# Eight bursts of small products in a gated recurrence gathered into two

## The chip, the cores and the metric

The kernel runs on one core of one Trainium2 chip. The metric is the time of one execution on the device in microseconds (us); less is better. Runs of this kernel lie within some 0.06% of each other, so a difference of about 0.2% (1.9 us) is what a measurement can tell from none.

## The reference, cut to what matters

Two transformer blocks with 256 tokens and a width of 1024, in float32. The change touches one mixer of the first block, a gated linear recurrence with 4 heads of 128 channels, worked in chunks of 64 tokens:

```python
f = lb + (1.0 - lb) * jax.nn.sigmoid(f_logit)
qh, kh, ih = heads(silu(q)), heads(1.0 - f), heads(i)
G = jnp.cumsum(heads(jnp.log(f)), axis=3)
def step(S, inp):
    qc, kc, ic, Gc = inp
    diff = Gc[:, :, :, None, :] - Gc[:, :, None, :, :]
    decay = jnp.exp(jnp.where(causal, diff, -jnp.inf))
    A = jnp.einsum('bhtc,bhsc,bhtsc->bhts', qc, kc, decay)
    o = einsum('bhts,bhsv->bhtv', A, ic) + einsum('bhtc,bhcv->bhtv', qc * jnp.exp(Gc), S)
    S_new = S * jnp.exp(G_last)[..., None] + einsum('bhsc,bhsv->bhcv', kc * jnp.exp(G_last - Gc), ic)
```

## The kernel before

Nearly all the work is projections of 256 tokens by streamed weights. A weight unit (1 MB) is loaded by SyncE's queue into one of three `raw` buffers, ScalarE rounds it to float32r (`Wh`, in `hi_to`, L1104), VectorE makes the rest (`Wl`, in `lo_to`, L1620), and TensorE sums three wide products for each (`three`, L418). Each engine's program is written out by hand in one order; semaphores join them. The two rings `Wh` and `Wl` hold three units, so ScalarE may start on unit u+2 of this stage when TensorE has ended unit u-1.

The attention matrix `A` of the recurrence is made without a chunk loop. For a block of 128 tokens it is split by halves of 1, 2, 4, ... 64 tokens: seven levels. In level n the later half of each pair of halves looks at the earlier half. `level_sub(n)` on VectorE writes differences of `G` into a buffer `E`, `level(n)` on ScalarE takes their exponential in place, `level_mul(n)` on VectorE multiplies them by keys and queries, `level_products(n)` on TensorE multiplies the halves (L698), and `level_out(n)` on VectorE copies what belongs to `A` out of the PSUM bank, for levels 0 to 4 into `Near`, for 5 and 6 into `Am`. The diagonal comes from `own_products` (L688) and `near_out`. ScalarE later copies `Near` into `Am` (L1264, four instructions). Then `cross_products` (L707) needs the chunk-to-chunk factors that `chunk_sub`, an exponential (L1271) and `chunk_mul` (L1866, L1867) make in `E1`, and `hgrn_out` (L724, L725) multiplies by the values.

None of this fills TensorE, so it is woven into the six gate projections: twelve weight units, u = 0 to 11, of 24 wide products each. After unit u TensorE calls `levels_after(u)`. At u = 0 that is the diagonal, at u = 1 to 7 level u-1. The loops `for u in range(12)` of ScalarE and VectorE have the steps that go with it in the same count. `gate_out(j)` on ScalarE reads a finished half of a gate out of PSUM, which frees its bank for a later unit. The levels take turns in two buffers `E`, and their products in the four PSUM banks of `T`. Products of the levels use 32 columns of the array at a time (64 in level 6), the projections 128. Each call on float32 data stands twice in the trace, with two loads of weights.

Of the kernel before, what the change touches and what calls it, by code (L numbers as in the profile page):

```python
# [9 lines left out]
ACT = mybir.ActivationFunctionType  # L10
# [5 lines left out]
HALVES = (1, 2, 4, 8, 16, 32, 64)  # L16
# [124 lines left out]
def heads(x, n):  # L141
    return x.rearrange("p (h d) -> p h d", h=n)


def build(nc, plan, I, out):
    ctx = ExitStack()
    with ctx:
        def sb(name, n, dt=F32, parts=128):
            return ctx.enter_context(nc.sbuf_tensor(name, [parts, n], dt))
# [19 lines left out]
        HG = sb("HG", 5 * 1024)  # L169
        Am, Ax = sb("Am", 1024), sb("Ax", 512)  # L170
        Iv, Sg, Vt, Vm = sb("Iv", 1024), sb("Sg", 1024), sb("Vt", 1024), sb("Vm", 1024)
        P = [sb(f"P{i}", 512) for i in range(2)]
        PT = [sb(f"PT{i}", 512) for i in range(2)]
        Near = PT[0][:, 0:256]
        onesr, DH, DL = sb("onesr", 128, F32R), sb("DH", 256, F32R), sb("DL", 256, F32R)
# [68 lines left out]
            return VT[:, ROWS[name] + i:ROWS[name] + i + 1]  # L244

        Q, K, G, E0, E1 = (HG[:, 1024 * j:1024 * j + 1024] for j in range(5))
        E = (E0, E1)

        forget_own, forget_keys = Iv, (Vm[:, :], G)
        forget_sums = nc.dram_tensor("forget_sums", [8, 256], F32).ap()  # L250
# [45 lines left out]
        def full(key):  # L296
            return ps_full[at[key][0]], at[key][1]

        def free(key):
            return ps_free[at[key][0]], at[key][2]  # L300
# [98 lines left out]
        def pe_program(pe):  # L399
# [280 lines left out]
            def own_products():  # L680
                b = T.take()
                pe.wait_ge(k_made, 1)
                pe.wait_ge(q_made, 2)
                t = take("kq", b)
                for q in range(8):
                    for x in range(0, 128, 32):
                        c = slice(q * 128 + x, q * 128 + x + 32)
                        ins = pe.matmul(t[x:x + 32, q * 32:q * 32 + 32], K[:, c], Q[:, c], start=True, stop=True)  # L688
                ins.then_inc(ps_full[b], 1)

            def level_products(n):
                pe.wait_ge(dec_mul, 2 * n + 2)
                b = T.take()
                t = take(("lv", n), b)
                for q in range(8):
                    s = E[n % 2][:, q * 128:q * 128 + 128]
                    for x, w, a, z in LEVELS[n]:
                        ins = pe.matmul(t[x:x + w, q * w + w - z:q * w + w], s[:, x:x + w], s[:, x + a:x + a + z],  # L698
                                        start=True, stop=True)
                ins.then_inc(ps_full[b], 1)  # L700
# [25 lines left out]
                    ins.then_inc(ps_full[6 + m], 1)  # L726

            def levels_after(u):
                if u == 0:
                    own_products()  # L730
                elif u < 8:
                    level_products(u - 1)
                elif u == 10:
                    hgrn_out()

# [356 lines left out]
        def act_program(act):  # L1092
# [134 lines left out]

            def level(n):
                act.wait_ge(dec_sub, 2 * n + 2)
                act.activation(E[n % 2], E[n % 2], ACT.Exp).then_inc(dec_exp, 1)  # L1230

            def gate_sigmoid(j):
                g = BIGT[:, j * 1024:j * 1024 + 1024]
# [12 lines left out]
            def gate_out(u):  # L1246
                c, m = u // 2, u % 2
                half_scaled(BIGT[:, c * 1024:c * 1024 + 1024], ("gate", c), m, rs0)

            level(0)  # L1250
            for u in range(12):
                hi_to(gate_unit(u) + 2)
                if u >= 2 and u % 2 == 0 and u < 8:
                    gate_out(u - 1)
                if u in (5, 6):
                    mem_squares(u - 5)
                if 1 <= u <= 6:
                    level(u)
                elif u == 7:
                    gate_out(6)  # L1260
                    gate_out(7)
                    act.wait_ge(*free(("lv", 4)))
                    for x in range(0, 128, 32):
                        act.activation(heads(Am[x:x + 32, :], 8)[:, :, x:x + 32], heads(Near[x:x + 32, :], 8),  # L1264
                                       ACT.Copy).then_inc(near_placed, 1)
                    for j in range(4):
                        gate_sigmoid(j)
                elif u == 8:
                    gate_out(8)
                    act.wait_ge(ch_sub, 4)  # L1270
                    act.activation(E1, E1, ACT.Exp).then_inc(ch_exp, 1)  # L1271
                    gate_out(9)
                elif u == 9:
                    act.wait_ge(*full("ax"))
                    act.wait_ge(lam_made, 1)
                    act.activation(Ax[:, :], bank[at["ax"][0]][:, :], ACT.Copy).then_inc(*emptied("ax"))
                elif u == 10:
                    for m in range(2):
                        act.wait_ge(*full(("ho", m)))
                        act.activation(P[m][:, :], bank[6 + m][:, :], ACT.Square).then_inc(ho_sq, 1)  # L1280
                if u in (1, 3, 5, 11):
                    gate_out(u - 1)
# [327 lines left out]
        def dve_program(dve):  # L1610
# [188 lines left out]

            def level_sub(n):  # L1800
                half = HALVES[n]
                v, g = (x.rearrange("p (a c b) -> p a c b", c=2, b=half) for x in (E[n % 2], G))
                end = g[:, :, 0, half - 1:half].to_broadcast([128, 512 // half, half])
                if n >= 2:
                    dve.wait_ge(*full(("lv", n - 2)))
                dve.tensor_tensor(v[:, :, 0, :], end, g[:, :, 0, :], ALU.subtract).then_inc(dec_sub, 1)
                if half < 64:
                    dve.tensor_tensor(v[:, :, 1, :], g[:, :, 1, :], end, ALU.subtract).then_inc(dec_sub, 1)
                else:
                    dve.tensor_copy(v[:, :, 1, :], g[:, :, 1, :]).then_inc(dec_sub, 1)  # L1810

            def level_mul(n):
                v, kv, qv = (x.rearrange("p (a c b) -> p a c b", c=2, b=HALVES[n]) for x in (E[n % 2], K, Q))
                dve.wait_ge(dec_exp, n + 1)
                dve.tensor_tensor(v[:, :, 0, :], v[:, :, 0, :], kv[:, :, 0, :], ALU.mult).then_inc(dec_mul, 1)
                dve.tensor_tensor(v[:, :, 1, :], v[:, :, 1, :], qv[:, :, 1, :], ALU.mult).then_inc(dec_mul, 1)
# [68 lines left out]
            for u in range(12):  # L1885
                lo_to(gate_unit(u) + (1 if u else 2))
                if 1 <= u < 7:
                    level_sub(u)
                if u == 0:
                    near_out("kq", 0, 0)  # L1890
                elif u < 7:
                    level_out(u - 1)
                    level_mul(u)
                elif u == 7:
                    level_out(6)
                elif u == 8:
                    chunk_sub()
                    lo_to(gate_unit(u) + 2)
                    chunk_mul()
                elif u == 10:  # L1900
                    hgrn_sums()
                if u:
                    lo_to(gate_unit(u) + 2)
# [660 lines left out]
```

## Time and profile before

| | us |
|---|---|
| median of three runs | 944.49 |
| lowest, highest | 944.22, 944.8 |
| profiled execution, whole | 944.71 |
| its span, first to last instruction | 942.8 |
| TensorE busy in the span | 935.6 |
| VectorE, ScalarE busy | 695.3, 526.8 |

The whole time of the profiled execution is 1.9 us more than its span. Busy shares count overlapping instructions once; the end of a matmul is modelled, so what a product costs is read from the distance of starts, not from its own duration.

### The profile page before, as it was taken

Reading aid. Unit: us, or ns where it says so; the run is one execution under the profiler, and the core shown is the slowest. Engines: PE = TensorE matmul, PEld = TensorE weight load, DVE = VectorE, ACT = ScalarE, POOL = GpSimd, SP = SyncE. Lnnn points to the kernel's source line nnn. Section 1 sums busy time; section 2 is a strip of 40 time slices with the busy share of each in tenths; the row PEclk is TensorE's granted clock in tenths of the full one; section 3 lists DMA queues with packets and bytes.
Section 4 is the critical chain, followed back from the end, with each engine's and each line's share of the span. In section 5 each row is a group of like instructions: output and inputs, shape, how many; then the busy total and the mean of one; then the engine's idle time right before and its main releaser. Section 6 shows DMA issues by size and latency. Waiting matters only on the chain.

```text
span 942.8 us, 13704 instructions
## 1 busy us (share of the span) xinstructions
PE 935.6 (99%) x5478; PEld 802.8 (85%) x5478; DVE 695.3 (74%) x1001; ACT 526.8 (56%) x673; POOL 80.9 (9%) x150
## 2 busy tenths in 40 slices
PE   9999999999999999999999999999999999999997
PEld 9988888888888888888888888888887888888886
DVE  6788668778768777788886757578878677576675
ACT  6676766654446556555655445356655465354544
POOL 1010228182100000000000000000003000000000
PEclk9999999999999999999999999999999999999999
DMA  9844555334564554556364554653534445646441
GB/s 360 332 157 161 176 182 221 135 135 161 186 239 179 184 193 166 217 179 223 135 230 172 197 205 178 223 179 135 182 134 171 164 144 213 222 155 221 160 179 45
DMA packets 26111, 175.10 MB, mean 186 GB/s; under 512 B 3256, under 2 KB 3520, under 8 KB 6080
## 3 DMA queue, kind: packets, MB, share of 16 engines
q1 hardware_dynamic: 25168, 170.15, 49.6%
q10 hardware_dynamic: 880, 4.07, 1.2%
q8 instruction: 44, 0.72, 0.3%
q14 instruction: 19, 0.16, 0.0%
HBM read 173.15 MB, written 1.06 MB: 185 GB/s over the span
## 4 chain that ended last, share of the span: by engine, by line
PE 99%; DVE 0%; ACT 0%; issue 0%; POOL 0%; ACTq 0%; POOLq 0%
PE ps L418 47%; PE ps L425 29%; PE ps L429 15%; PE ps L548 1%; PE ps L646 1%; PE ps L774 1%; PE ps L790 1%; PE ps L825 1%; PE ps L698 1%; PE ps L637 0%; PE ps L758 0%; PE ps L839 0%; PE ps L805 0%; PE ps L725 0%; PE ps L874 0%; PE ps L724 0%
## 5 line engine op out<-in xcount | busy, mean ns | idle before, releaser
L1620 DVE TENSOR_TENSOR Wl<-raw,Wh 128x2048 fp32r<-128x2048 f32 x151 | 346.2, 2295 | 32.1 <-ACT Wh L1104 31.5
L1104 ACT ACTIVATE Wh<-raw 128x2048 fp32r<-128x2048 f32 x154 | 294.4, 1913 | 31.8 <-PE ps L418 27.8
L425 PE MATMUL ps<-hT,Wh 128*128 128x512 f32 x1184 | 282.4, 391 | 0.0
L425 PEld LDWEIGHTS ps<-hT,Wh 128*128 128x128 f32 x1184 | 220.0, 188 | 45.4 <-issue 1.0
L418 PE MATMUL ps<-Wh,hT 128*128 128x512 f32 (+1 forms) x640 | 199.7, 385 | 0.0
L429 PEld LDWEIGHTS ps<-hT,Wl 128*128 128x128 f32 x1184 | 150.7, 191 | 4.3
L429 PE MATMUL ps<-hT,Wl 128*128 128x256 f32 x1184 | 153.8, 283 | 0.0
L418 PEld LDWEIGHTS ps<-Wh,hT 128*128 128x128 f32 x640 | 118.3, 188 | 23.8 <-issue 1.5
L1446 ACT ACTIVATE Am<-ps 128x512 f32<-128x512 f32 x66 | 39.1, 593 | 177.3 <-PE ps L429 173.8
L1709 DVE TENSOR_TENSOR PT<-ps,Am 128x256 f32<-128x256 f32 x132 | 49.7, 418 | 105.6 <-ACT Am L1446 105.6
L418 PE MATMUL ps<-Wh,yTh 128*128 128x512 f32 (+1 forms) x314 | 122.8, 391 | 0.0
L418 PE MATMUL ps<-Wl,yTh 128*128 128x512 f32 (+1 forms) x314 | 122.2, 389 | 0.0
L418 PE MATMUL ps<-Wh,yTl 128*128 128x512 f32 (+1 forms) x314 | 121.8, 388 | 0.0
L418 PE MATMUL ps<-Wl,hT 128*128 128x512 f32 (+1 forms) x320 | 121.4, 379 | 0.0
L418 PEld LDWEIGHTS ps<-Wh,yTl 128*128 128x128 f32 x314 | 59.0, 188 | 12.4
L418 PEld LDWEIGHTS ps<-Wl,hT 128*128 128x128 f32 x320 | 60.3, 188 | 10.3
L418 PEld LDWEIGHTS ps<-Wh,yTh 128*128 128x128 f32 x314 | 59.1, 188 | 11.5 <-issue 0.3
L418 PEld LDWEIGHTS ps<-Wl,yTh 128*128 128x128 f32 x314 | 59.1, 188 | 10.8
L2343 POOL TENSOR_SCALAR sm<-sm 128x8 f32<-128x8 f32 (+3 forms) x8 | 3.6, 453 | 522.9 <-DVE sm L2249 466.6
L1495 ACT ACTIVATE yTh<-PT 128x512 fp32r<-128x512 f32 x33 | 20.8, 632 | 42.3 <-DVE PT L2166 39.2
L1331 ACT ACTIVATE P<-ps,sm 128x256 f32<-128x256 f32 (+1 forms) x56 | 23.2, 427 | 24.7 <-DVE sm L1965 13.3
L2160 DVE TENSOR_TENSOR P<-P,RB 128x512 f32<-128x512 f32 x33 | 22.7, 687 | 7.0 <-ACT P L1477 7.0
(257 smaller groups left out, 815.9 us busy)
## 6 DMA issues: line engine op xcount, KB each, us to landing
raw<-in_units SPq DMA_DIRECT2D x154, 1024.0 KB, 4.8
FP<-in_bias ACTq DMA_DIRECT2D x1, 2048.0 KB, 11.1
FP<-in_first SPq DMA_DIRECT2D x2, 768.0 KB, 8.2
FP<-in_first SPq DMA_DIRECT2D x3, 384.0 KB, 5.4
raw<-in_units SPq DMA_DIRECT2D x2, 512.0 KB, 10.1
X<-in_x SPq DMA_DIRECT2D x1, 1024.0 KB, 16.7
Hn<-in_mem SPq DMA_DIRECT2D x1, 1024.0 KB, 9.0
XT<-in_mem_turned SPq DMA_DIRECT2D x1, 1024.0 KB, 11.0
```

The costliest lines, as they stand in the source:

```text
L418: ins = pe.matmul(o, l(k), r(k), start=first and k == ks[0] and j == 0, stop=last and k == ks[-1] and j == 2)
L425: pe.matmul(o, lh(k), hT_both(k), start=first and k == ks[0], stop=False)
L429: ins = pe.matmul(o[:, 256:512], ll(k), hT_at(k)[0], start=False, stop=last and k == ks[-1])
L548: ins = pe.transpose(t[:, q * 128:q * 128 + 128], src[:, m * n + k * 128:m * n + k * 128 + 128], ident)
L646: ins = pe.matmul(ts[m][c][:, 0:z - a], x[:, m * 128:m * 128 + 128], w[:, k, a:z], start=begin, stop=end)
L1104: act.activation(wh[j % NS][:, 0:n], raw[j % NR][:, 0:n], ACT.Copy).then_inc(w_hi, 1)
L1331: act.activation(P[i % 2][:, x:z], t[:, x:z], ACT.Exp, bias=mn[:, c], scale=-1.0, accum_out=den[:, c]).then_inc(*(emptied(key) if m else s ...
L1446: act.activation(v3(crossed_out(n)), t, ACT.Copy).then_inc(cross_made, 1)
L1495: act.activation(yTh[:, j % 2 * 512:j % 2 * 512 + 512], g[:, :], ACT.Copy).then_inc(y_hi, 1)
L1620: dve.tensor_tensor(wl[j % NS][:, 0:n], raw[j % NR][:, 0:n], wh[j % NS][:, 0:n].bitcast(F32), ALU.subtract).then_inc(w_lo, 1)
L1709: dve.tensor_tensor(d[:, m, :], t[:, m, :], v3(crossed_out(n))[:, m, :], ALU.add).then_inc(*emptied((key, key + ("x",))[m]))
L2160: dve.tensor_tensor(v3(c), v3(c), by_token(2), ALU.mult).then_inc(act_made, 1)
```

## The change

The diagonal and levels 0, 1 and 2 are all multiplied after unit 3, and levels 3 to 6 after unit 7; after units 0, 1, 2, 4, 5 and 6 TensorE goes straight on. For that the levels get four buffers: `E0`, `E1`, `Vt` and a tile `PP`, which is the former two tiles `P` in one piece. `level_sub` now waits for the products of level n-4, not n-2. VectorE copies the diagonal and level 0 out at its u = 4, levels 1 and 2 at 5 and 6, and 3 to 6 together at 8. ScalarE's four copies of `Near` move from u = 7 to u = 8, behind the exponential for the chunks.

```diff
-        E = (E0, E1)
+        E = (E0, E1, Vt[:, :], PP[:, :])
...
             def levels_after(u):
-                if u == 0:
-                    own_products()
-                elif u < 8:
-                    level_products(u - 1)
+                if u in (3, 7):
+                    if u == 3:
+                        own_products()
+                    for n in range(3) if u == 3 else range(3, 7):
+                        level_products(n)
...
                 elif u == 8:
                     gate_out(8)
                     act.wait_ge(ch_sub, 4)
                     act.activation(E1, E1, ACT.Exp).then_inc(ch_exp, 1)
+                    act.wait_ge(*free(("lv", 4)))
+                    for x in range(0, 128, 32):
+                        act.activation(heads(Am[x:x + 32, :], 8)[:, :, x:x + 32], heads(Near[x:x + 32, :], 8),
+                                       ACT.Copy).then_inc(near_placed, 1)
                     gate_out(9)
...
-                if n >= 2:
-                    dve.wait_ge(*full(("lv", n - 2)))
+                if n >= 4:
+                    dve.wait_ge(*full(("lv", n - 4)))
...
-                if u == 0:
+                if u == 4:
                     near_out("kq", 0, 0)
-                elif u < 7:
-                    level_out(u - 1)
+                    level_out(0)
+                elif u in (5, 6):
+                    level_out(u - 4)
+                if 1 <= u < 7:
                     level_mul(u)
-                elif u == 7:
-                    level_out(6)
                 elif u == 8:
+                    for n in range(3, 7):
+                        level_out(n)
                     chunk_sub()
```

TensorE's row of instructions before, from the diagonal after unit 0 (L688) to level 0 after unit 1 (L698); L418 are wide products of the gates:

```order
276 L418 MATMUL ps<-Wh,hT 128x512
277 L688 MATMUL ps<-HG 32x32 x32
278 L418 MATMUL ps<-Wh,hT 128x512
...
294 L418 MATMUL ps<-Wh,hT 128x512
295 L698 MATMUL ps<-HG 32x31 x32
296 L418 MATMUL ps<-Wh,hT 128x512
```

TensorE's row with the change, around units 3 and 7 (its L689 is L688 of before, L699 is L698, L419 is L418):

```order
324 L419 MATMUL ps<-Wh,hT 128x512
325 L689 MATMUL ps<-HG 32x32 x32
326 L699 MATMUL ps<-HG 32x31 x32
327 L699 MATMUL ps<-HG 32x30 x32
328 L699 MATMUL ps<-Vt 32x28 x32
329 L419 MATMUL ps<-Wh,hT 128x512
...
393 L419 MATMUL ps<-Wh,hT 128x512
394 L699 MATMUL ps<-PP 32x24 x32
395 L699 MATMUL ps<-HG 32x16 x32
396 L699 MATMUL ps<-HG 32x32 x16
397 L699 MATMUL ps<-Vt 64x64 x8
398 L419 MATMUL ps<-Wh,hT 128x512
```

Eight bursts between wide products have become two, of four groups each.

VectorE's row before, at its u = 0 and 1: the multiplication of level 0 (L1815, L1816), the diagonal's copy (L1822), the subtraction of level 1 (L1806, L1808), the copy of level 0, the multiplication of level 1:

```order
64 L1816 TENSOR_TENSOR HG<-HG 128x512
65 L1822 COPY_PREDICATED PT<-masks,ps 128x256
66 L1806 TENSOR_TENSOR HG<-HG 128x256x2
67 L1808 TENSOR_TENSOR HG<-HG 128x256x2
68 L1822 COPY_PREDICATED PT<-masks,ps 128x8x31
69 L1815 TENSOR_TENSOR HG<-HG 128x256x2
70 L1816 TENSOR_TENSOR HG<-HG 128x256x2
```

The same place with the change, each line two higher in number, with the weight unit 3 (L1622) behind it:

```order
64 L1818 TENSOR_TENSOR HG<-HG 128x512
65 L1808 TENSOR_TENSOR HG<-HG 128x256x2
66 L1810 TENSOR_TENSOR HG<-HG 128x256x2
67 L1817 TENSOR_TENSOR HG<-HG 128x256x2
68 L1818 TENSOR_TENSOR HG<-HG 128x256x2
69 L1622 TENSOR_TENSOR Wl<-raw,Wh 128x2048
```

The two copies have left this place; nothing in it reads a bank of TensorE any more.

## Rows read from the trace of the kernel before

**Rows 1.** The page: busy time and share of TensorE; shares of the chain that ended last.

```profile
PE 935.6 (99%) x5478; PEld 802.8 (85%) x5478; DVE 695.3 (74%) x1001; ACT 526.8 (56%) x673; POOL 80.9 (9%) x150
PE 99%; DVE 0%; ACT 0%; issue 0%; POOL 0%; ACTq 0%; POOLq 0%
```

**Rows 2.** Waits of the weight loads (PEld): line, waited for: us, times, longest.

```profile
PEld ps L698 <- issue: 2.5, 7, 0.4
```

**Rows 3.** Chain in order of time: start, us, what; a stretch without small products.

```profile
255.01 13.62 PE ps L418 x60
```

**Rows 4.** Timeline of TensorE around level 0: start, us, line, out<-in, count.

```profile
62.87 0.39 PE L418 MATMUL ps<-Wh,hT 128*128 128x512 f32 x1
63.19 0.76 PE L698 MATMUL ps<-HG 128*32 128x31 f32 x64
63.88 0.50 PE L418 MATMUL ps<-Wh,hT 128*128 128x512 f32 x1
64.22 0.39 PE L418 MATMUL ps<-Wl,hT 128*128 128x512 f32 x1
```

**Rows 5.** The same timeline around level 5 and level 6.

```profile
94.64 0.39 PE L418 MATMUL ps<-Wh,hT 128*128 128x512 f32 x1
94.95 0.70 PE L698 MATMUL ps<-HG 128*32 128x32 f32 x32
...
95.92 0.39 PE L418 MATMUL ps<-Wl,hT 128*128 128x512 f32 x1
...
100.93 0.39 PE L418 MATMUL ps<-Wh,hT 128*128 128x512 f32 x1
101.25 1.15 PE L698 MATMUL ps<-HG 128*64 128x64 f32 x16
...
102.66 0.39 PE L418 MATMUL ps<-Wl,hT 128*128 128x512 f32 x1
```

**Rows 6.** Line L698: durations in ns (least/median/most) of the small products.

```profile
L698 PE MATMUL ps<-HG x368: 182/194/270, 63.2 to 102.2; 128*32 128x31 f32 x32, 128*32 128x30 f32 x32, 128*32 128x28 f32 x32, 128*32 128x24 f32 x32
```

**Rows 7.** Line L406, TensorE's waits for a free bank, 55 to 125 us.

```profile
L406 PEldq EVENT_SEMAPHORE  x12: 51/51/51, 59.0 to 111.5; - x12
```

**Rows 8.** Timeline of TensorE: the last wide product of unit 0.

```profile
56.49 0.39 PE L418 MATMUL ps<-Wh,hT 128*128 128x512 f32 x1
```

**Rows 9.** Timelines of VectorE and of ScalarE at levels 0 and 1.

```profile
61.12 0.45 DVE L1822 COPY_PREDICATED PT<-masks,ps 128x256 f32<-128x256 uint8 x1
61.46 0.69 DVE L1806 TENSOR_TENSOR HG<-HG 128x512 f32<-128x512 f32 x1
62.06 0.69 DVE L1808 TENSOR_TENSOR HG<-HG 128x512 f32<-128x512 f32 x1
...
65.59 2.28 DVE L1620 TENSOR_TENSOR Wl<-raw,Wh 128x2048 fp32r<-128x2048 f32 x1
...
62.78 1.06 ACT L1230 ACTIVATE HG<-HG 128x1024 f32<-128x1024 f32 x1 [2.06 <-DVE HG L1808]
```

**Rows 10.** Timelines of ScalarE, VectorE and TensorE from unit 7 to the chunk products.

```profile
101.94 1.72 ACT L1264 ACTIVATE Am<-PT 32x256 f32<-32x256 f32 x4
...
110.82 0.69 ACT L1143 ACTIVATE FP<-ps,sm 128x512 f32<-128x512 f32 x1
...
113.78 0.67 ACT L1143 ACTIVATE FP<-ps,sm 128x512 f32<-128x512 f32 x1
...
110.71 2.29 DVE L1620 TENSOR_TENSOR Wl<-raw,Wh 128x2048 fp32r<-128x2048 f32 x1 [3.99 <-ACT Wh L1104]
...
115.34 0.28 DVE L1867 TENSOR_TENSOR HG<-HG 128x128 f32<-128x128 f32 x1
...
116.06 1.05 PE L707 MATMUL ps<-HG 128*128 128x128 f32 x8
116.86 0.48 PE L418 MATMUL ps<-Wh,hT 128*128 128x512 f32 x1
```

**Rows 11.** The page, DMA queues: the queue that brings instructions; packets, MB, share of 16 engines.

```profile
q8 instruction: 44, 0.72, 0.3%
```

More of the change, by code:

```diff
@@ L171, in build @@
         Iv, Sg, Vt, Vm = sb("Iv", 1024), sb("Sg", 1024), sb("Vt", 1024), sb("Vm", 1024)
-        P = [sb(f"P{i}", 512) for i in range(2)]
+        PP = sb("PP", 1024)
+        P = [PP[:, 512 * i:512 * i + 512] for i in range(2)]
         PT = [sb(f"PT{i}", 512) for i in range(2)]
@@ L695, in level_products @@
                 for q in range(8):
-                    s = E[n % 2][:, q * 128:q * 128 + 128]
+                    s = E[n % 4][:, q * 128:q * 128 + 128]
                     for x, w, a, z in LEVELS[n]:
@@ L1229, in level @@
                 act.wait_ge(dec_sub, 2 * n + 2)
-                act.activation(E[n % 2], E[n % 2], ACT.Exp).then_inc(dec_exp, 1)
+                act.activation(E[n % 4], E[n % 4], ACT.Exp).then_inc(dec_exp, 1)
             def gate_sigmoid(j):
@@ L1261, in act_program @@
                     gate_out(7)
[L1262 to L1265, printed above, removed]
                     for j in range(4):
@@ L1801, in level_sub @@
                 half = HALVES[n]
-                v, g = (x.rearrange("p (a c b) -> p a c b", c=2, b=half) for x in (E[n % 2], G))
+                v, g = (x.rearrange("p (a c b) -> p a c b", c=2, b=half) for x in (E[n % 4], G))
                 end = g[:, :, 0, half - 1:half].to_broadcast([128, 512 // half, half])
-                if n >= 2:
-                    dve.wait_ge(*full(("lv", n - 2)))
+                if n >= 4:
+                    dve.wait_ge(*full(("lv", n - 4)))
                 dve.tensor_tensor(v[:, :, 0, :], end, g[:, :, 0, :], ALU.subtract).then_inc(dec_sub, 1)
@@ L1812, in level_mul @@
             def level_mul(n):
-                v, kv, qv = (x.rearrange("p (a c b) -> p a c b", c=2, b=HALVES[n]) for x in (E[n % 2], K, Q))
+                v, kv, qv = (x.rearrange("p (a c b) -> p a c b", c=2, b=HALVES[n]) for x in (E[n % 4], K, Q))
                 dve.wait_ge(dec_exp, n + 1)
```

## The prediction, as it was put on record

> **What bounds the kernel now.** I read the busy shares first, then the chain, then what TensorE waits for. TensorE is busy for 935.6 of 942.8 us and the chain that ended last is 99% TensorE; no other engine has a share of it [rows 1]. So only what TensorE spends counts, plus any wait that the change puts in front of it. Among its own waits the small products of the recurrence stand out, 2.5 us in 7 times with "issue" as the releaser, which means that no other engine was waited for [rows 2]. Something between the wide and the small products costs time by itself. That is the stage to read: 56 to 123 us.
>
> **What a burst costs now.** In a stretch of wide products alone one takes 13.62 / 60 = 0.227 us from start to start [rows 3]. Around level 0 the last wide product starts at 62.87 and the second one behind the burst at 64.22 [rows 4]. Two steps of 0.227 lie in these 1.35 us, so the burst costs 1.35 - 0.45 = 0.90 us. Its 64 small products run in 0.76 us less the 0.19 that the last one takes by itself [rows 4, 6], so they start within 0.57 us, 9 ns apart. The remaining 0.32 is **going in and coming out**: 0.09 in front (0.32 between the starts where 0.23 is usual), the rest behind, where the first wide product starts late and the second one 0.34 after it [rows 4]. Level 5 costs 1.28 - 0.45 = 0.83, of which its 32 products take 0.70 - 0.20 + 0.02 = 0.52; 0.31 is left. Level 6 costs 1.73 - 0.45 = 1.28, of which its 16 products take about 1.15 - 0.23 + 0.06 = 0.98; 0.30 is left [rows 5]. So each burst pays about 0.31 us for the two changes of shape, whatever is in it. The diagonal and levels 1 to 4 look like level 0.
>
> **What the change removes.** Eight bursts become two, with the same products. Six times in and out are gone: 6 x 0.31 = 1.86 us. That is the ceiling, since the small products themselves stay.
>
> **What it adds on TensorE.** Inside a burst there are three joints, six in all, which the trace of before does not show: a group of small products directly behind another. Each has a wait for a free bank, which takes the sequencer 51 ns [rows 7], and a wait for VectorE's products. From below a joint costs nothing, because TensorE still has queued work to run while the sequencer is at the wait, and no reason gives a gain, since the products keep their 9 ns. From above it costs what a whole way in and out costs now, 0.31 us, and then nothing is won. Five joints lie between groups of 32 columns, and the nearest row is the 51 ns wait, so I take 0.05 each, 0.25 together. The last one, from 32 columns to the 64 of level 6, changes the shape as the way in does; I take that price, 0.09, rounded to 0.1. Together 0.35, with ends 0 and 1.86.
>
> The Trainium skill (Trainium TensorE Tiling (Array Packing), Key Properties) says that changing the tiling mode, and not merely the tile, drains the array. No row of before has two groups of small products together, so it can't be held against one. By that rule alone the five joints of one mode would be free and the sum would be 1.86 - 0.1 = 1.76 us.
>
> **What it moves on VectorE and ScalarE.** This must stay under TensorE's own work, and TensorE now asks earlier: without a burst after units 0 to 2, it comes to unit 3 sooner. The last product of unit 0 starts at 56.49 [rows 8]; 0.23 later unit 1 starts, and 48 steps of 0.227 further unit 3, at 67.6. It needs VectorE's `lo_to` of that unit, 65.59 to 67.87 before [rows 9]. In front of that the copy of the diagonal, 61.12 to 61.46, and the copy of level 0 are gone. The subtraction of level 1 thus starts at 61.12 and ends at 62.4 (two steps of 0.60, the last 0.69); the exponential of 1.06 starts some 0.03 later and ends at 63.5; two multiplications of 0.6 bring 64.8, and `lo_to` is done at 64.8 + 2.28 = 67.1. That is 0.5 us early (0.3 by the load of the weights, which starts a step before). The cover is thin: it costs 0.1 us for each 0.1 us of lateness. After unit 3 the burst of some 2.6 us lets VectorE get ahead again, and a unit takes it about 6 us where TensorE takes 5.5. Behind unit 7, `level_out` 3 to 6 stand in front of `chunk_sub`, but the latter was early by more than 4 us (VectorE waited 3.99 us for ScalarE until 110.71, [rows 10]), so four copies of 0.3 to 0.9 us are covered.
>
> ScalarE's four copies of `Near`, 1.72 us, leave the place in front of `gate_out(8)`, which TensorE released anyway at 110.82, and stand behind the exponential. The chain to the chunk products, `gate_out(8)`, table, exponential, `chunk_mul`, is the same as before: its last multiplication ended at 115.62 and TensorE began at 116.06 [rows 10], and both ends shift with TensorE. Behind it `gate_out(9)` comes 1.72 later: 113.78 + 1.72 + 0.67 = 116.17 in the old clock, and its bank is needed at 116.86 [rows 10], so 0.7 us are left. `hgrn_out` needs `Near` only some 3.6 us behind the chunk products. I cost all of this at nothing; if the three thin covers go, at up to 0.2 to 0.5 us each.
>
> **The sum.** 1.86 - 0.35 = 1.5 us less. The profiled execution took 944.71, so 943.2; it stood 0.2 over the median of the runs, 944.49, so the **forecast is 943.0 us**. About 0.2%, 1.9 us, is what a measurement can tell from no change; the forecast lies within that.
>
> **Rival one, the joints cost as much as the ways in and out.** If the 0.31 comes from a semaphore wait on the weight load, and not from the change of shape, every joint keeps it: 6 x 0.31 given back, 944.5. For it speaks that each burst starts with such a wait. Against it, each weight unit begins with a wait as well, and in the stretch without small products these sit among steps of 0.227 [rows 3]. Partly so, with the thin covers lost as well, it gives 944 to 945.
>
> **Rival two, the joints are free.** Then 944.5 - 1.86 = 942.6, on the border of what can be told. Only if the small products also start closer together in a long burst does it go under that; nothing in the rows shows them faster than 9 ns.
>
> **Rival three, instructions come too late, and it is slower.** A group of 64 products is 128 instructions with its weight loads. The first burst holds 4 x 128 = 512 and the second 128 + 128 + 64 + 32 = 352. The queue for instructions brought 44 packets for 2 x 5478 [rows 1, 11], so about 250 in each, and a packet took 0.003 x 16 x 942.8 / 44 = 1.0 us. The two bursts use up about 3.5 packets, at 1.15 us each in the first burst. In the wide stream one lasts 28 us. If the engine held no packet ahead, 3.5 x 1.0 would lie bare: 943.0 + 3.5 = 946.5, slower by 0.2%. It decides from one and a half bare packets on; below that the gain is larger. Against it: bursts of 128 go at 9 ns now, half a packet at once, and no burst is slower than the others.
>
> The Trainium skill (Runtime: NRT & Kernel Launch, Instruction fetch mechanics) speaks on both sides: fetching is hidden because instructions are dispatched slower than they arrive, at about 20 cycles each, which at 2.4 GHz I estimate at 8 ns, and the burst has two in 9 ns [rows 4]. The same page gives TensorE room for 2048 instructions; by that the 512 would be there, nothing would be lost, and the sum stays at 943.0. No row of before shows how much is held.
>
> **How the numbers follow.** The forecast's own case, 942.6 to 943.7, has 0.66; rival one, 943.7 to 945, 0.16; rival two taken below 942.6, 0.10; rival three 0.08. The range reaches from the free joints with 0.2 of scatter, 942.4, to all joints paid, 944.5, and leaves out rival three and a part of rival one. Faster by over 0.2% 0.10, within 0.82, slower 0.08.
>
> **What would show it.** In the changed kernel's timeline two bursts should stand, of about 2.4 and 2.8 us from first to last start, each with 0.32 between the starts in front and 0.34 behind, and groups inside one following each other within 0.1 us. "Issue" waits on L698 should fall from 7 to one or two. A step of 0.3 between groups would be rival one; a hole of 0.5 us or more within a group, rival three. A wait of TensorE for VectorE's `Wl` at unit 3 or for the chunk products would show a thin cover gone. The forecast is wrong in kind if TensorE's idle time grows anywhere after 123 us.

## The result, and the profile after

The changed kernel takes 946.53 us (median of 17 runs, 944.93 to 949.36); the kernel before, measured beside it, 944.55 (17 runs, 944.12 to 945.18). The ratio is 1.0022, with 1.0016 to 1.0028 as its 95% interval. It is slower by 2.0 us, where 1.5 less was forecast, and its runs lie 4.4 us apart, those of before 1.1. The profiled execution took 946.41, its span 944.5.

Two lines of the page answer to [rows 1]: TensorE is as full as before and the chain is still TensorE alone. What is new stands in its waits. The two rows with PE are all waits of its products, the one with PEld is that of the small products' weight loads, as in [rows 2] (line, waited for: us, times, longest).

```profile
PE 935.4 (99%) x5478; PEld 804.1 (85%) x5478; DVE 695.3 (74%) x1001; ACT 527.1 (56%) x673; POOL 82.7 (9%) x150
PE 99%; issue 0%; DVE 0%; ACT 0%; POOL 0%; ACTq 0%; POOLq 0%
```

```profile
PE ps L699 <- issue: 2.0, 1, 2.0
PE ps L638 <- POOL ones L2360: 1.0, 1, 1.0
PEld ps L699 <- issue: 2.4, 2, 2.1
```

One wait of 2.0 us on the small products (L699 is L698 of before), with "issue" as its releaser: no other engine was waited for. The waits of the weight loads fell from 7 to 2, as forecast, and one of the two is the same hole. The timeline of TensorE around both bursts (start, us, line, out<-in, count, idle time in front) answers to [rows 4, 5]:

```profile
72.27 0.39 PE L419 MATMUL ps<-Wh,hT 128*128 128x512 f32 x1
72.58 0.76 PE L689 MATMUL ps<-HG 128*32 128x32 f32 x64
73.20 1.39 PE L699 MATMUL ps<-HG 128*32 128x31 f32 x128
74.45 0.75 PE L699 MATMUL ps<-Vt 128*32 128x28 f32 x64
75.13 0.50 PE L419 MATMUL ps<-Wh,hT 128*128 128x512 f32 x1
75.47 0.40 PE L419 MATMUL ps<-Wl,hT 128*128 128x512 f32 x1
...
97.04 0.39 PE L419 MATMUL ps<-Wh,hT 128*128 128x512 f32 x1
97.36 0.75 PE L699 MATMUL ps<-PP 128*32 128x24 f32 x64
97.99 1.29 PE L699 MATMUL ps<-HG 128*32 128x16 f32 x96
99.20 0.97 PE L699 MATMUL ps<-Vt 128*64 128x64 f32 x13
102.16 0.33 PE L699 MATMUL ps<-Vt 128*64 128x64 f32 x3 [1.99 <-issue]
102.42 0.50 PE L419 MATMUL ps<-Wh,hT 128*128 128x512 f32 x1
102.76 0.40 PE L419 MATMUL ps<-Wl,hT 128*128 128x512 f32 x1
...
103.46 0.60 PE L419 MATMUL ps<-Wl,hT 128*128 128x512 f32 x1
103.86 1.05 PE L419 MATMUL ps<-Wh,hT 128*128 128x512 f32 x2
104.71 0.63 PE L419 MATMUL ps<-Wl,hT 128*128 128x512 f32 x1
```

Three things are to be read from it.

**The gain is there.** From the last wide product to the second one behind, less two usual steps of 0.227, the first burst costs 75.47 - 72.27 - 0.45 = 2.75 us. Its four parts, read in the same way, cost 0.89 + 0.89 + 0.89 + 0.89 = 3.57 before. The second costs 102.76 - 97.04 - 0.45 = 5.27; without 2.15 of hole it is 3.12, where levels 3 to 6 cost 0.88 + 0.87 + 0.83 + 1.27 = 3.85. Together 1.55 us saved.

**A hole lies inside level 6**, after 13 of its 16 products. From the start of the thirteenth at 99.95 to 102.16 are 2.21 us, where 0.06 is usual (0.98 of [rows 5] over 16): 2.15 lost.

**The wide products behind it are slow.** The two at 103.86 and the one at 104.71 start 0.427 apart, and so on to 107.11: 3.65 us for nine steps, which take 2.04 elsewhere. 1.6 us are lost. The table of stretches (us, busy time of each engine, granted clock in parts of 2.4 GHz, DMA share, GB/s) shows the clock there at its lower level, 1.2 GHz, and back at full behind:

```profile
99.90:102.10 2.20, 0.28 (x5) 0.19 (x4) 0.28 (x1) 2.20 (x3) 0.00 (x0) 1.00 0.96 398
103.40:106.90 3.50, 3.50 (x10) 2.69 (x10) 2.92 (x5) 1.76 (x1) 0.00 (x0) 0.51 0.02 5
107.10:110.60 3.50, 3.50 (x17) 2.86 (x16) 0.39 (x1) 0.00 (x0) 0.00 (x0) 1.00 0.64 185
```

In the hole itself the clock was granted in full, with TensorE nearly empty; it fell some 1.3 us after work had come back. Behind the first burst two wide products lost 0.2 us together. So 2.15 + 1.6 + 0.2 - 1.55 = 2.4 us should be lost. The same wide products, compared between the two traces, give 2.3: the last one of unit 0, in front of all that was changed, starts 0.54 us earlier here (55.95 against 56.49), and one behind both bursts 1.74 later (111.68 against 109.94). The span grew by 1.7.

**Whose instructions were late.** TensorE's instructions arrive in packets of 256: its 11218 in the trace, waits included, go with the 44 packets of 16 KB in [rows 11]. Counted in the built program, the first burst is instructions 926 to 1441, with the waits, and packets begin at 961, 1217 and 1473; the second is 1636 to 1991, and packets begin at 1729 and 1985. 1985 is the fourteenth product of level 6, the very place of the hole. The packets of the queue for instructions, read one by one from the packed trace, against TensorE's resumption at such a border (us):

```
kernel                   packet began, landed   TensorE resumes   landing to resumption
changed, first burst       71.65    72.58         73.98   (0.03 late)   1.40
changed, behind it         76.67    77.61         79.00   (0.1 late)    1.39
changed, level 6           99.78   100.78        102.16   (2.15 late)   1.38
changed, second run       102.49   103.46        104.88   (3.99 late)   1.42
```

Each time the products start again 1.4 us after a packet has landed, whether they were held by 0.03 us or by 4 (the second run is the unchanged kernel, e8 below). That ties the hole to the packet. In the second burst the sequencer passed the border 1729 at about 97.8, 93 instructions into the burst; the packet for 1985 began 2 us later and was usable 4.4 us after that border, and the burst had come to 1985 after 2.2. In the first burst the border 961 lies only 35 instructions in: the sequencer, which runs ahead in the wide stream, had passed it before the first small product, the packet began at 71.65, and the stall shrank to 0.03 us. It isn't always so small: at the same place, behind the 145th product of the first burst, e4's trace lost 0.17, e8's 0.31, e6's 0.45 and e2's 0.62 us (starts less the usual 0.009), with products again 1.31 to 1.41 us after the landing.

### The profile page after: what moved, and what is told of

Its sections match the earlier page's. It is cut to its first block, busy times and chain, and to the rows that moved or that the text cites. A ratio compares the mean times of both kernels' runs of the same rounds, so it can differ in the third digit from the quotient of the medians.

```text
span 944.5 us, 13704 instructions
## 1 busy us (share of the span) xinstructions
PE 935.4 (99%) x5478; PEld 804.1 (85%) x5478; DVE 695.3 (74%) x1001; ACT 527.1 (56%) x673; POOL 82.7 (9%) x150
## 4 chain that ended last, share of the span: by engine, by line
PE 99%; issue 0%; DVE 0%; ACT 0%; POOL 0%; ACTq 0%; POOLq 0%
PE ps L419 47%; PE ps L426 29%; PE ps L430 15%; PE ps L549 1%; PE ps L647 1%; PE ps L776 1%; PE ps L792 1%; PE ps L827 1%; PE ps L699 1%; PE ps L638 0%; PE ps L760 0%; PE ps L841 0%; PE ps L807 0%; PE ps L726 0%; PE ps L876 0%
## 5 line engine op out<-in xcount | busy, mean ns | idle before, releaser
L1622 DVE TENSOR_TENSOR Wl<-raw,Wh 128x2048 fp32r<-128x2048 f32 x151 | 345.9, 2294 | 30.7 <-ACT Wh L1106 30.1
L419 PE MATMUL ps<-Wh,hT 128*128 128x512 f32 (+1 forms) x640 | 199.2, 386 | 0.0
L419 PEld LDWEIGHTS ps<-Wh,hT 128*128 128x128 f32 x640 | 119.1, 189 | 23.9 <-issue 1.5
L419 PE MATMUL ps<-Wh,yTh 128*128 128x512 f32 (+1 forms) x314 | 122.8, 391 | 0.0
L419 PE MATMUL ps<-Wl,hT 128*128 128x512 f32 (+1 forms) x320 | 122.2, 382 | 0.0
L419 PE MATMUL ps<-Wl,yTh 128*128 128x512 f32 (+1 forms) x314 | 122.1, 389 | 0.0
L419 PE MATMUL ps<-Wh,yTl 128*128 128x512 f32 (+1 forms) x314 | 121.8, 388 | 0.0
L419 PEld LDWEIGHTS ps<-Wl,hT 128*128 128x128 f32 x320 | 60.6, 189 | 11.0 <-issue 0.3
L419 PEld LDWEIGHTS ps<-Wh,yTl 128*128 128x128 f32 x314 | 59.0, 188 | 12.4
L419 PEld LDWEIGHTS ps<-Wh,yTh 128*128 128x128 f32 x314 | 59.1, 188 | 11.5 <-issue 0.3
L419 PEld LDWEIGHTS ps<-Wl,yTh 128*128 128x128 f32 x314 | 59.1, 188 | 10.8
L1333 ACT ACTIVATE PP<-ps,sm 128x256 f32<-128x256 f32 (+1 forms) x56 | 23.2, 427 | 24.7 <-DVE sm L1969 13.3
L2164 DVE TENSOR_TENSOR PP<-PP,RB 128x512 f32<-128x512 f32 x33 | 22.7, 687 | 7.0 <-ACT PP L1479 7.0
```

The source lines that it names most:

```text
L419: ins = pe.matmul(o, l(k), r(k), start=first and k == ks[0] and j == 0, stop=last and k == ks[-1] and j == 2)
L1333: act.activation(P[i % 2][:, x:z], t[:, x:z], ACT.Exp, bias=mn[:, c], scale=-1.0, accum_out=den[:, c]).then_inc(*(emptied(key) if m else s ...
L1622: dve.tensor_tensor(wl[j % NS][:, 0:n], raw[j % NR][:, 0:n], wh[j % NS][:, 0:n].bitcast(F32), ALU.subtract).then_inc(w_lo, 1)
L2164: dve.tensor_tensor(v3(c), v3(c), by_token(2), ALU.mult).then_inc(act_made, 1)
```

## The experiments

The theories put on record with them: H, a burst stalls when a border of packets inside it is followed by a whole packet of small products; and as rivals, that the hole belongs to level 6 itself or its data, that the long bursts make the clock fall, and that the memory traffic of the two loads side by side makes the hole.

### e1: the program shifted by 64 instructions

```diff
+            pad(32)
             rows_out(("hq", 1), WF)
+            pad(32)
```

`pad(n)` is n empty instructions on TensorE, each with two waits on a semaphore that has its value long since.

> The changed kernel with 64 empty waits added to TensorE's program ahead of the gate projections (32 in front of and 32 behind the second query projection). They cost nothing by themselves, since TensorE has queued work. They shift where in the instruction stream each instruction stands by 64, a quarter of the 256 that one packet of the instruction queue brings. Theory (the sequencer runs out of instructions): the block border that now stands 6 instructions before the end of the second burst comes to lie 38 earlier than level 6, in level 5, with the border before it close to that burst's start, and one border comes to lie 32 before the end of the first burst. So the 2.2 us hole leaves level 6; a hole of about 3 us stands in the first burst, in level 2; time about 947 to 948. Rival one (the hole belongs to level 6, its 64 columns or its tile Vt): it stays in level 6, about 946.5. Rival two (a wait for another engine): it stays between the same instructions, 946.5.

948.33 us against 944.83 for before, ratio 1.0040 (1.0027 to 1.0054). TensorE's timeline around the first burst (L705 is L699):

```profile
77.54 0.61 PE L705 MATMUL ps<-Vt 128*32 128x28 f32 x48
80.14 0.33 PE L705 MATMUL ps<-Vt 128*32 128x28 f32 x16 [1.98 <-issue]
...
104.21 1.15 PE L705 MATMUL ps<-Vt 128*64 128x64 f32 x16
```

Level 6 is whole, and the hole stands in level 2, after 48 of 64 products, 32 instructions before the burst's end. That is where the count of 256 puts it, and it lost 2.2 us where 3 were expected; the level, its data and its 64 columns have nothing to do with it. The time can't be used: contrary to the expectation the pads cost something themselves, since TensorE waited for `Wl` early on (`DVE Wl L1628`, 2.6 us in 2 times).

### e2 and e3: 216 empty instructions between the bursts, and the same in the kernel before

```diff
+                    if u in (4, 6):
+                        pad(54)
...
+                if c in (2, 3):
+                    pad(54)
```

> The changed kernel with 216 empty waits in TensorE's program between its first and its second burst, 54 at each of four places. Theory (instructions come too late): the borders of the second burst move so that only one lies in it, 133 in, and the next 34 behind its end; the first burst keeps its place. No hole of over 0.3 us in either burst, no slow wide products behind the second, and the time that was forecast, 943.0 (942.6 to 943.6). Rivals (the hole belongs to level 6 or to a wait): the hole of 2.2 us in level 6 stays, 946.5.

> The kernel before with the same 216 empty waits at the same four places. It shows what they cost by themselves. Theory: nothing, 944.5 (within 0.3), with the levels' bursts as before. If they cost something, the result of the run with the two bursts has to be read against this one.

956.83 us (1.0127, 1.0112 to 1.0143) for the changed kernel with pads, 962.60 (1.0190, 1.0176 to 1.0204) for the kernel before with them. The pads are dear, which I had taken as nearly free, so the time of neither says what was asked. The kernel before with pads (L702 is L698, L418 as ever), with the hole behind a burst, and the stretch that follows:

```profile
76.41 0.76 PE L702 MATMUL ps<-HG 128*32 128x28 f32 x64
82.95 0.76 PE L418 MATMUL ps<-Wh,hT 128*128 128x512 f32 x1 [5.79 <-issue]
```

```profile
83.50:88.60 5.10, 5.10 (x13) 3.95 (x12) 0.00 (x0) 0.00 (x0) 0.00 (x0) 0.50 0.34 138
```

Two things are still of use. The second burst of e2, moved off its border, ran through level 6 without a hole (`x16` in one piece at 114.02); the first was held for the 0.62 us told above, where no hole over 0.3 was expected. And a kernel without any long burst has the slow wide products too, as soon as it has a hole: 0.50 of the clock for these 5 us.

### e4: three bursts of 512, 256 and 96 instructions

```diff
-                    for n in range(3) if u == 3 else range(3, 7):
-                        level_products(n)
+                for n in {3: (0, 1, 2), 5: (3, 4), 7: (5, 6)}.get(u, ()):
+                    level_products(n)
```

> The changed kernel with the second burst cut in two: levels 3 and 4 after unit 5, levels 5 and 6 after unit 7; the first burst as in the change; no empty waits. Theory (instructions come too late when a burst uses up more than a block within the time that a block needs to arrive): at most one border lies in either of the new bursts, 128 in, and the next over 100 instructions later, so no hole; five ways in and out are saved at 0.31, less four joints at 0.05 and one at 0.1: 944.5 - 1.25 = 943.2. Rival (the hole belongs to level 6 behind level 5, or to waits on the levels): a hole of about 2 us stays in level 6, and the time is about 946.5.

943.83 us (11 runs) against 944.83, ratio 0.9988 (0.9979 to 0.9997), where 943.2 was expected. No hole in the two later bursts; level 6 lies at the same count in the program as in the changed kernel, border and all, and runs in one piece:

```profile
99.73 0.70 PE L699 MATMUL ps<-HG 128*32 128x32 f32 x32
100.36 1.15 PE L699 MATMUL ps<-Vt 128*64 128x64 f32 x16
```

So a border in a burst need not cost anything by itself. Here the 256 instructions in front of it hold two weight units of wide products, and the packet had landed long before. The first burst kept the changed kernel's products and their order, and no slow clock followed it.

### e6: the second burst half a weight unit earlier

```diff
-                if u in (3, 7):
-                    if u == 3:
-                        own_products()
-                    for n in range(3) if u == 3 else range(3, 7):
+                if u == 3:
+                    own_products()
+                    for n in range(3):
                         level_products(n)
...
+                if c == 3:
+                    mids[1, 0] = lambda: [level_products(n) for n in range(3, 7)]
```

> The changed kernel with its second burst half a unit earlier: behind the third quarter of the fourth gate's projection (24 instructions before its place), all else alike. The block border that stood 6 instructions before the burst's end now stands 18 behind it, the one before it 117 in. Theory (instructions come too late): TensorE has 9 wide products queued, 2.0 us, when the sequencer stops, so most or all of the 2.2 us hole is covered; a remainder of 0 to 0.8 us may stand between wide products behind the burst. Time 943.0 to 944.0. Rival (the hole belongs to level 6 or to four levels in a row): the hole stays in level 6, 946.5. Rival two (VectorE's level 6 is then waited for): a wait for VectorE in front of level 6, 943.5 to 945.

**943.22 us** (11 runs, 942.67 to 944.04) against 944.70, ratio 0.9984 (0.9976 to 0.9993), 1.48 us less. The burst is the same in every product; only its place against the borders is another, 24 instructions earlier, so that the border behind its 256 instructions falls 18 behind its end, among wide products that wait in TensorE's queue.

```profile
95.25 0.39 PE L419 MATMUL ps<-Wh,hT 128*128 128x512 f32 x1
95.56 0.75 PE L699 MATMUL ps<-PP 128*32 128x24 f32 x64
96.17 1.29 PE L699 MATMUL ps<-HG 128*32 128x16 f32 x96
97.39 1.15 PE L699 MATMUL ps<-Vt 128*64 128x64 f32 x16
98.46 0.50 PE L419 MATMUL ps<-Wh,hT 128*128 128x512 f32 x1
98.80 0.39 PE L419 MATMUL ps<-Wl,hT 128*128 128x512 f32 x1
```

It costs 98.80 - 95.25 - 0.45 = 3.10 us, the changed kernel's 3.12 without the hole. This second burst is the forecast's case as it was worked out, and the kernel the fastest of all that ran. Two things belong beside it. Its first burst was still held, at the border of the changed kernel:

```profile
73.91 0.93 PE L699 MATMUL ps<-HG 128*32 128x31 f32 x81
75.10 0.61 PE L699 MATMUL ps<-HG 128*32 128x30 f32 x47 [0.26 <-issue]
```

And its packet came sooner. It began at 97.04, 1.0 us behind the border 117 in, and landed at 98.38, so that it could be used by 99.8, before the nine wide products behind the burst were through (about 100.6). With the changed kernel's 2.0 us to the start it would have been about as late as those nine allow, so the place accounts for nearly all of it, but the trace doesn't part the two.

### e7: levels 3 to 6 multiplied twice

```diff
-                for q in range(8):
+                for q in list(range(8)) * (2 if n >= 3 else 1):
```

> The changed kernel with levels 3 to 6 multiplied twice each into the same bank, so that the second burst has about 707 instructions and three block borders, 93, 349 and 605 in. Theory (instructions come too late): more holes: at the border 349 in, of 2 to 3 us, and at that 605 in one of about 3 us, since 256 instructions there last 1.2 us and a block took some 4.4 us from its border to use; with 1.6 us of products more 943.0 + 1.6 + 5 to 6 = 949.5 to 951, more where the clock falls. Rival (one hole for level 6): one hole of 2.2 us and 1.6 of products, 948.

951.70 us (4 runs, 950.30 to 955.51) against 944.70, ratio 1.0079 (1.0056 to 1.0102). Two holes:

```profile
99.69 0.58 PE L699 MATMUL ps<-HG 128*32 128x16 f32 x46
103.12 2.56 PE L699 MATMUL ps<-HG 128*32 128x16 f32 x128 [2.85 <-issue]
106.46 0.75 PE L699 MATMUL ps<-HG 128*32 128x32 f32 x18 [0.77 <-issue]
```

Between the first and the second stand 128 products, 256 instructions with their weight loads. The first lies in level 4 now. The second is shorter since the clock was at 0.50 between them and the products took 2.3 us to use up a packet, twice as long as at full clock. Its packet also began sooner, at 104.16, 1.0 us after the products had come back, where the first one had taken 1.8; a hole of 3 us was expected. Holes sit at packets, and their length is what the packet has left to arrive when the products are through.

### e5, e9, e10: a hole in the kernel before, without any long burst

```diff
                 elif u < 8:
                     level_products(u - 1)
+                    if u == 7:
+                        for _ in range(40):
+                            pe.wait_ge(ones_set, 1)
```

40, 60 and 92 such waits, two to an instruction: 20, 30 and 46 empty instructions behind level 6.

> The kernel before with 20 empty wait instructions (two conditions that hold in each) right behind level 6's products after unit 7, where TensorE has no work queued. In the run with 54 of them one stretch left TensorE idle for about 6 us, so some 0.11 us each: here a hole of about 2.2 us that has nothing to do with instruction packets. Theory: the two costs of the changed kernel are separate, the hole itself and the granted clock that falls to half behind it in some executions; then this run costs 2.2 us by itself, 946.7, and up to 1.6 more where the clock falls behind the hole for some 3.5 us, so 946.7 to 948.5 with a wider scatter than before. Rival (the lower clock belongs to the long burst of small products and not to the hole): 946.7 with the scatter of before, 0.5, and no slow wide products behind the hole.

> The kernel before with 30 empty wait instructions behind level 6's products, in place of 20. 20 made a hole of 1.24 us, since the sequencer was about 0.9 us ahead, and 54 one of 6: at 0.108 us each, 30 leave a hole of about 2.3 us, as long as in the changed kernel's first trace. Theory (the granted clock falls behind a hole in some executions, whatever made it): a mean cost of 2.3 to 4, so 947.0 to 948.7, with a scatter of 2 us or more between executions, as the changed kernel has. Rival (the fall needs a long burst of small products): 947.0, scatter 0.5 as before.

> The same with 46 empty wait instructions: a hole of about 4.0 us, as long as in the second trace of the changed kernel. Theory: 4.0 for the hole and 1.5 to 2 for the clock in most executions, 948.7 to 950.7, with slow wide products behind the hole in the trace, 0.43 from start to start. Rival: 948.7 with wide products at 0.227.

The holes came out at 1.17, 2.29 and 4.02 us (one empty instruction takes 0.108, and the first nine or so are covered by what TensorE has queued). The first wide products behind each, e5, e9, e10 in turn (each kernel's own timeline), and at the end the later part of the last hole and the stretch behind it, with the granted clock:

```profile
103.92 0.47 PE L418 MATMUL ps<-Wh,hT 128*128 128x512 f32 x1 [1.17 <-issue]
104.22 0.40 PE L418 MATMUL ps<-Wl,hT 128*128 128x512 f32 x1
104.46 0.39 PE L418 MATMUL ps<-Wh,hT 128*128 128x512 f32 x1
```

```profile
105.20 0.47 PE L418 MATMUL ps<-Wh,hT 128*128 128x512 f32 x1 [2.29 <-issue]
...
106.41 0.63 PE L418 MATMUL ps<-Wl,hT 128*128 128x512 f32 x1
106.84 0.63 PE L418 MATMUL ps<-Wh,hT 128*128 128x512 f32 x1
```

```profile
106.47 0.77 PE L418 MATMUL ps<-Wh,hT 128*128 128x512 f32 x1 [4.02 <-issue]
```

```profile
104.80:106.40 1.60, 0.00 (x0) 0.00 (x0) 1.57 (x6) 1.59 (x3) 0.00 (x0) 0.50 0.11 20
107.00:110.00 3.00, 3.00 (x8) 2.32 (x7) 0.00 (x0) 3.00 (x4) 0.00 (x0) 0.50 0.72 298
```

In time: 945.62 (1.0010, 1.0002 to 1.0019), 947.63 (1.0031, 1.0021 to 1.0042, runs 3.2 us apart) and 950.98 (1.0067, 1.0054 to 1.0080), against 944.70 and 944.73. The hole of e5 came out at half its expected length, and so its time lies under what was expected: it costs 0.9 us, less than itself, and no slow products follow it. That of 4.0 costs 6.25, a little over what was expected: itself and about 2.2 more, which is what the lower clock takes. That of 2.3 lies between, and its runs fall in two: four with a mean granted clock of 0.999 take 946.61 to 946.94, four with 0.997 take 948.32 to 949.78. All runs of e4, of e5, of e6 and of the kernel before beside them have 0.998 or more; all five of e10 have 0.997 or less, and so have 12 of the 23 of the changed kernel (e8 with them). So the slow stretch follows a hole, whatever made it, and long bursts whose holes stay under 0.5 us (e4, e6) have none. It doesn't follow every time: behind e1's hole of 1.98 and e11's of 1.99 the wide products kept their 0.23.

### e8: the changed kernel once more

No edit.

> The changed kernel once more, in the company of these runs. Theory: again a hole inside level 6, 13 products in, about 2 us long, with a packet of the instruction queue landing 1.4 us before its end; behind it the granted clock may fall or not. 945 to 948. Rival (the hole of the first trace is an accident of one execution): no hole, 943.

948.57 us (6 runs, 945.37 to 949.79) against 944.70, ratio 1.0036 (1.0022 to 1.0049). The hole is at the same product, but nearly twice as long:

```profile
100.08 0.97 PE L699 MATMUL ps<-Vt 128*64 128x64 f32 x13
104.88 0.33 PE L699 MATMUL ps<-Vt 128*64 128x64 f32 x3 [3.83 <-issue]
```

Its place is fixed by the program; its length is not. Here the packet began only at 102.49, some 4 us behind the border, where it was 2 in the first trace. The clock stood at 0.57 from 105 to 109. The length of the hole and the clock behind it are the two things in the traces that differ, which fits the scatter of the runs.

### e11: one load at a time

In the changed kernel VectorE makes two units of `Wl` one after the other (L1622, twice 2.29 us from 93.07), so two loads of 1 MB are issued 2.2 us apart, at 95.38 and 97.58, and the DMA engines are 0.97 busy from 97.0 to 99.8, when the packet should come; before, 0.28 in 97.0 to 102.3. Here the second is put behind `level_out` 3 to 6.

```diff
-                lo_to(gate_unit(u) + (1 if u else 2))
+                if u != 8:
+                    lo_to(gate_unit(u) + (1 if u else 2))
...
                     for n in range(3, 7):
                         level_out(n)
+                    lo_to(gate_unit(u) + 1)
...
-                if u:
+                if u and u != 7:
```

> The changed kernel with one step of VectorE moved: the low part of the weight unit for unit 9 is made behind the copies of levels 3 to 6, not in front of them. That step allows a weight load of 1 MB, which in the changed kernel is issued 2.5 us behind another one and fills the DMA engines to 97% during the second burst. Here one load at a time is under way. Theory (the packet of instructions comes late because it shares the DMA engines with two loads): the hole in level 6 stays at the same instruction, but is shorter, 0.5 to 1.5 us in place of 2.2 and 4.1, and fewer executions have the lower clock: 944 to 945.5. Rival (a packet takes its 4 us whatever the DMA engines do): the hole is 2 us or more and the time 946.5 to 948.5 as before.

945.54 us (median of 11 runs: ten of 944.99 to 946.84, and one of 1561.34 at a granted clock of 0.556, whose cause no run shows) against 944.56, ratio 1.0013 (1.0003 to 1.0022). In the trace the second load is gone from behind, and the hole is as long as ever:

```profile
97.00:100.00 3.00, 3.00 (x165) 2.49 (x165) 0.62 (x2) 1.61 (x2) 0.96 (x5) 1.00 0.86 292
100.00:103.00 3.00, 1.10 (x26) 0.97 (x19) 0.90 (x3) 2.99 (x4) 0.00 (x0) 1.00 0.16 63
```

```profile
100.13 0.97 PE L699 MATMUL ps<-Vt 128*64 128x64 f32 x13
103.08 0.33 PE L699 MATMUL ps<-Vt 128*64 128x64 f32 x3 [1.99 <-issue]
```

The expectation of a shorter hole is missed: the second load isn't what sets the 2.0 us. The first one is still there, though, and this run can't clear it. Compare what the DMA engines did between the border and the start of the packet here, up to 100.25, and in e1, where the product at the border stands at 76.76 and the packet began at 77.77:

```profile
98.66:100.25 1.59, 1.59 (x138) 1.55 (x128) 0.70 (x3) 1.57 (x2) 0.00 (x0) 1.00 1.00 422
76.76:77.77 1.01, 1.01 (x127) 1.01 (x120) 1.01 (x1) 1.01 (x2) 0.00 (x0) 1.00 0.00 0
```

The DMA share is 1.00 here and 0.00 there. With the engines full the packet began 1.8 to 2.0 us behind the border (the changed kernel's first trace, e7's first, e11), 3.8 in e8; with them idle or nearly so 1.0 (e1, e6, and e7's second packet at a share of 0.21). So the traffic goes with 1 to 3 us of the hole in these traces; no run changes it alone.

The median is 1.0 lower than the changed kernel's against before (0.98 above it, where that has 1.98 and in e8 3.87), and the sum fits a hole with no slow clock behind it: 944.56 - 1.55 + 2.15 + 0.2 = 945.4. That fewer executions have the lower clock, as expected, fits the runs: 3 of these ten have a granted clock of 0.997 or less, 12 of the 23 of the changed kernel. That less traffic keeps the longer holes away is possible; one trace for each can't show it.

## Why the prediction was wrong

**The bound, right.** Only what TensorE spends counted; the loss stands in its own timeline.

**The ceiling and the joints, right in size.** 1.86 less 0.35 was 1.5; measured were 1.55 in the trace, and 1.48 in time in e6, whose trace still has 0.45 of hole in its first burst. From the last start of one group to the first of the next are 0.04 to 0.07 us, so 0.03 to 0.06 over the usual 0.009, where 0.05 was taken; the joint to the 64 columns of level 6 is 0.126, 0.12 over, where 0.1 was taken. Rival one, a joint at 0.31, falls: six would have left nothing of the 1.55. Rival two's sum was 1.86; the joints are not free. TensorEngine Tiling (Array Packing) of the Trainium skill, Key Properties, lets only a change of mode drain the array, by which the five would be free. The trace has 0.03 to 0.06 in each, and the measurement decides; whether that is the 51 ns wait in front of each [rows 7], no run shows.

**The covers, right.** `lo_to` for unit 3 ended at 66.49, before TensorE asked; no wait of TensorE for `Wl` or for the chunk products stands in its list of waits above. Behind unit 7 VectorE's last multiplication for the chunks began at 117.08 and took 0.28, the chunk products began at 117.80.

**The weighing of rival three, wrong; this is the step that failed.** The sum has no term for instructions that come late, and the rival that does got 0.08, on two grounds. The first was that "bursts of 128 go at 9 ns now, half a packet at once, and no burst is slower than the others". A burst of 128 can't show it. A packet that is asked for at one border is needed at the next, 256 instructions on, and with bursts of 128 these 256 always hold a whole unit of 24 wide products, 24 x 0.227 = 5.4 us; the packet needed 4.4. The rows spoke for bursts of the old length only, and I read them as speaking for four times that. The second was the price: 3.5 packets at 1.0 us each, of which one and a half had to lie bare. The 1.0 us was right for the transfer (99.78 to 100.78), but it isn't what a late packet costs. From border to use there are 2.0 us (3.8 in e8) before it begins, 1.0 of transfer and 1.4 behind; against this stand the 1.15 us in which a burst of 32 columns uses up a packet, 2.2 where level 6 is in it. At five borders, one packet that came 2 us late was enough. The time of 946.5 was met by an accident of sizes: 2.15 + 0.2 for the packets and some 1.2 more in the median, for the longer holes and the lower clock, which no step of the prediction had.

**What should have been asked.** [rows 11] give the size of a packet. With it the borders can be counted in the built program, and the question is then whether a packet's worth of small products follows one. In e6's second burst the answer is no, by 18 instructions. In the first burst it is yes too. Where its border lies 35 instructions in, as in the changed kernel, the packet began before the first small product and the lateness was 0 to 0.6 us; in e1, where it lies 227 in, 2.2.

Of what is held ahead, the runs show this: a hole stands at the first border that has 256 fast instructions between it and the border in front (the changed kernel's level 6, e1, e7, and small ones in the first burst), which is what one packet at work and one asked for at the border would do. Runtime: NRT & Kernel Launch of the Trainium skill, Instruction fetch mechanics, gives TensorE room for 2048 instructions and calls the fetch mostly hidden; the same section also speaks of two lines of 256. The measured holes, 256 instructions apart in e7, agree with the latter and not with the former.

**What stays open.** Why a packet begins 1 us behind its border in one execution, 2 in another and 3.8 in a third: the traffic on the DMA engines goes with it in the traces under e11, but no run moves the traffic alone. And why the clock falls behind one hole of 2 us and not behind another.

## What to carry to other kernels

Gathering small products pays the price of each change of shape that it removes (0.31 us here), as long as no whole packet of instructions is used up inside a burst while the next one is still on its way. Count the borders in the built program, 256 instructions apart, and keep the second border of a burst outside it, or have slow work in front; moving the burst by 24 instructions was worth about 3.5 us here, from 2.0 above the kernel before to 1.5 below it (5.4 against e8, which was measured beside it). Such a placement is undone by any later edit that adds instructions in front of it, so it has to be counted anew each time.

## What the hardware showed unexpectedly

- From the landing of a packet of instructions to the first product out of it 1.30 to 1.44 us, in holes of 0.03 to 4 us alike (eight traces).
- Behind a hole TensorE may run at 0.50 of its clock: from 1.3 us behind the hole of 2.2 us for 3.4 us (the changed kernel, up to 1.6 us lost), from 0.5 behind that of 4 in e8, and in e10 from inside the hole, so that all twelve steps behind it, 106.47 to 111.66, were slow (2.4 us lost). Behind e1's and e11's holes of 2 us and e5's of 1.2 it stayed at 1.00.
- An empty instruction with two waits that are met long since takes 0.108 us on TensorE, twice the 51 ns of a wait in [rows 7], and hides only behind what is queued there: 216 of them cost the kernel before 18 us, the lower clock behind the holes included.
